# One block, two reserved tiles of expert 0, and the low parts of expert 0's first matrices computed ahead of the step plan

## What is computed

```python
def hier_moe(x, w_router_group, w_router_expert, moe_w1, moe_w3, moe_w2):
...
    p_grp = jax.nn.softmax((xt @ w_router_group).astype(jnp.float32), axis=-1)
    g_idx = jnp.argmax(p_grp, axis=-1)
...
    top_v, top_i = lax.top_k(e_logits, TOP_K_INNER)
    top_w = jax.nn.softmax(top_v, axis=-1) * g_gate
    expert_id = g_idx[:, None] * EXPERTS_PER_GROUP + top_i
...
    h = jax.nn.silu(jnp.einsum('nd,edf->nef', xt, moe_w1)) * jnp.einsum('nd,edf->nef', xt, moe_w3)
    h = h * gates.astype(h.dtype)[..., None]
    y = jnp.einsum('nef,efd->nd', h, moe_w2)
    return y.reshape(shp)
...
    x = layer_norm(ALPHA * x + m, ln1_g, ln1_b)
    x = layer_norm(ALPHA * x + hier_moe(x, w_router_group, w_router_expert, moe_w1, moe_w3, moe_w2),
                   ln2_g, ln2_b)
```

## Time and profile before

| what | us |
|---|---|
| median of three runs | 1213.25 (1211.74 to 1216.63) |
| profiled execution, first to last instruction | 1221.8 |
| end of the first block (PE L801, DVE goes on) | 750.3 |
| plan copied | 764.3 |
| output product of step 1 begins | 794.6 |
| PE busy | 1127.9 (92%) |
| DVE busy | 808.8 (66%) |
| ACT busy | 538.7 (44%) |

### The profile page before, as it was taken

The page is one execution under the profiler, slowest core; times in us unless marked ns, Lnnn a source line. Parts: engine busy times, 40 slices in busy tenths (PEclk is TensorE's granted clock), DMA queues, the critical chain, the costliest instruction groups (busy, mean ns, idle before and its releaser), DMA issues. The chain is left out here.

```text
span 1221.8 us, 20871 instructions
## 1 busy us (share of the span) xinstructions
PE 1127.9 (92%) x5734; PEld 998.6 (82%) x5735; DVE 808.8 (66%) x1530; ACT 538.7 (44%) x703; POOL 188.0 (15%) x189
## 2 busy tenths in 40 slices
PE   6999999999999999999999985899998999999970
PEld 6999999999999999788888864677887887777750
DVE  5666455464346556667777766866755798888884
ACT  4465344443344444323222224444544676656530
POOL 1000000000001001002223313315001033221322
PEclk9999999999999999999999997899998999999995
DMA  5331597768776444524444228676766789788563
GB/s 184 124 105 57 134 138 131 76 155 98 92 83 217 189 159 152 197 69 139 149 161 172 105 63 273 234 267 208 265 230 245 271 309 356 292 294 294 192 223 137
DMA packets 86989, 221.08 MB, mean 181 GB/s; under 512 B 18992, under 2 KB 45648, under 8 KB 80656
## 3 DMA queue, kind: packets, MB, share of 16 engines
q1 hardware_dynamic: 57824, 129.90, 32.3%
q0 software_dynamic: 18160, 59.53, 14.6%
q10 hardware_dynamic: 10944, 30.95, 13.5%
HBM read 133.75 MB, written 86.58 MB: 180 GB/s over the span
## 5 line engine op out<-in xcount | busy, mean ns | idle before, releaser
L1462 PE MATMUL ps_h<-x_hi,xt_hi 128*128 x320 | 128.6, 402 | 2.7 <-issue 1.8
L1462 PE MATMUL ps_h<-x_hi,xt_lo 128*128 x320 | 125.0, 391 | 0.0
L1462 PE MATMUL ps_h<-w_lo,xt_hi 128*128 x320 | 124.9, 390 | 0.0
L287 PE MATMUL ps_vb_c<-x_hi,w_hi 128*128 (+1 forms) x320 | 114.6, 358 | 10.6 <-DVE x_lo L461 10.6
L287 PE MATMUL ps_vb_c<-x_hi,w_lo 128*128 (+1 forms) x320 | 113.9, 356 | 0.0
L287 PE MATMUL ps_vb_c<-x_lo,w_hi 128*128 (+1 forms) x320 | 113.2, 354 | 0.0
L287 PE MATMUL ps_va_b<-x_hi,w_lo 128*128 (+1 forms) x320 | 112.7, 352 | 0.0
L287 PE MATMUL ps_va_b<-x_hi,w_hi 128*128 (+1 forms) x320 | 112.6, 352 | 0.0
L287 PE MATMUL ps_va_b<-x_lo,w_hi 128*128 (+1 forms) x320 | 111.8, 349 | 0.0
L1119 DVE TENSOR_TENSOR w_lo<-x_hi_p,x_hi 128x2048 f32 (+1 forms) x32 | 73.1, 2286 | 7.3 <-ACT x_hi L1114 5.6
L476 DVE SCALAR_TENSOR_TENSOR xc<-vb,par,xc 128x416 f32<-128x416 f32 (+1 forms) x60 | 39.1, 652 | 56.1 <-ACT xc L348 52.3
(11 more groups left out here) (356 smaller groups left out, 2656.1 us busy)
## 6 DMA issues: line engine op xcount, KB each, us to landing
x_hi_p<-in_w SPq DMA_DIRECT2D x48, 1024.0 KB, 5.1
o_scr<-x_raw ACTq DMA_DIRECT2D x42, 512.0 KB
w_lo_p<-xs_scr SPq DMA_DIRECT2D x41, 512.0 KB
o_scr<-w_lo_p SPq DMA_DIRECT2D x41, 512.0 KB
w_raw<-in_w_in POOLq DMA_DIRECT2D x19, 512.0 KB, 3.7
xs_scr<-x_raw ACTq DMA_DIRECT2D x17, 512.0 KB
x_raw<-in_x_t SPq DMA_DIRECT2D x20, 416.0 KB, 3.4
x_hi_p<-y_scr SPq DMA_DIRECT2D x16, 512.0 KB, 4.1
```

The source lines that it names most:

```text
L287: mm = pe.matmul(ps[i][:, 0:CHUNK], w[:, i, k], x[:, k, bass.ds(c * CHUNK, CHUNK)], start=(k == 0 and n == 0), stop=(k == KT - 1 and n == 2))
L1462: mm = pe.matmul(ps_h[par][:], x[:, par, k], w[:, bass.ds(at, 1), k].rearrange("p o n -> p (o n)"), start=(k == 0 and n == 0), stop=(k == ...
```

## The change

The two blocks become one: the engines' functions of the first phase (`project_*`) are called at the head of those of the second, with three hooks (`ahead`, `between`) through which work of the experts stands inside the first phase. Two tiles of expert 0 are reserved in place of one (FROZEN = 2), and both hidden products are computed with `first_part` ahead of the plan, the low parts of the matrix among them. SP loads both tiles' rows ahead of expert 0's matrices; the gates of the last two groups have a semaphore of their own (`s_gl`). On DVE `lo13` and the second `x_lo` stand ahead of `plan_steps`, `lo2` ahead of the copy of the plan. `later_experts` goes to step 1 and takes a scan and a subtraction over from `ranks`, which goes to step 2; `slots` goes to step 3, `records` and `needed` to step 4. Line numbers move by some ten lines.

```diff
+FROZEN = 2
...
-        dve.memset(self.start[:, 0:1], float(P))
-        self.then(dve, dve.tensor_scalar(self.run[:, 0:1], self.run[:, 0:1], float(P), None, ALU.max))
+        dve.memset(self.start[:, 0:1], float(FROZEN * P))
+        self.then(dve, dve.tensor_scalar(self.run[:, 0:1], self.run[:, 0:1], float(FROZEN * P), None, ALU.max))
...
-                                    self.wts[0:rows, t, c:c + 1], None).then_inc(self.s_gs, 16)
+                                    self.wts[0:rows, t, c:c + 1], None).then_inc(self.s_gs if n < len(GROUPED) - 2 else self.s_gl, 16)
...
-            sp.wait_ge(s_m, NT)
-            for half in (0, 1):
-                sp.dma_start(ew.raw_half(half), w13[0][:, half * (KT // 2):(half + 1) * (KT // 2)]).then_inc(ew.s_r13[half], 16)
-            sp.dma_start(ew.w2_raw[:], w2[0]).then_inc(ew.s_r2, 16)
-            sp.dma_start(ew.ln2[:], ln[:, 2:4]).then_inc(ew.s_ln2, 16)
-            sp.wait_ge(mx.s_st_out, 16)
-            for n in range(LAST - 5, LAST - 1):
-                sp.wait_ge(rt.s_sc[n % 4], rt.landed(n))
-            sp.wait_ge(rt.s_gs, 16 * TOPK * GROUPED[LAST - 1][0])
-
-        @block.tensor
-        def _(pe):
+        def project_tensor(pe, ahead):
...
+            ahead()
...
             scores(NT - 1)
...
+                if t == NT - 1:
+                    ahead()
                 act.wait_ge(s_tr, t + 1)
...
+            between()
             both_parts(NT - 1)
...
+            between()
             logits_out(NT - 1)
...
+            project_sync(sp)
+            for n in range(LAST - 5, LAST - 1):
+                sp.wait_ge(rt.s_sc[n % 4], rt.landed(n))
+            for par in range(FROZEN):
+                sp.dma_start(xg[:, par], xs_scr[par * P:(par + 1) * P, :]).then_inc(s_xg[par], 16)
+            sp.wait_ge(handover.s_m, NT)
+            for half in (0, 1):
+                load_weights(sp, 0, half)
+            load_weights(sp, 0)
+            sp.dma_start(ln2, ln[:, 2:4]).then_inc(ew.s_ln2, 16)
+            sp.wait_ge(rt.s_gs, 16 * TOPK * GROUPED[LAST - 1][0])
+            sp.wait_ge(handover.s_rt, NT)
             sp.dma_start(consts[:, 0:NCONST], consts_in).then_inc(s_con, 16)
-            sp.dma_start(gate[:, slot(0, 0)], g_scr[0:P, :]).then_inc(s_g[0], 16)
+            for par in range(FROZEN):
+                sp.dma_start(gate[:, slot(par, 0)], g_scr[par * P:(par + 1) * P, :]).then_inc(s_g[par], 16)
+            sp.wait_ge(handover.s_st_out, 16)
             sp.wait_ge(s_plan, 1)
             for n in (LAST - 1, LAST):
                 sp.wait_ge(rt.s_sc[n % 4], rt.landed(n))
-            ahead = [load(1, 1), load(2, 0)]
+            ahead = load(2, 0)
             next_weights(sp, 1)
-            sp.wait_ge(rt.s_gs, 16 * TOPK * NT)
-            load_gate(1, 1, 0, ahead[0])
-            load_gate(2, 0, 1, ahead[1])
+            sp.wait_ge(rt.s_gl, 16 * TOPK * (NT - GROUPED[LAST - 1][0]))
+            load_gate(2, 0, 1, ahead)
...
+            project_gpsimd(pool)
             for n in (LAST - 1, LAST):
                 rt.scatter(pool, n)
...
             def count_later():
 
                 pe.wait_ge(s_later, 1)
-                of = later.rearrange("p t e -> p (t e)")
-                pe.matmul(ps_o[1][:, 0:NT * NE], consts[:, C_TRI:C_TRI + P], of, start=True, stop=True)
-                pe.matmul(ps_o[0][:, 0:NT * NE], consts[:, C_ONE:C_ONE + P], of, start=True, stop=True).then_inc(s_cnt2, 1)
+                pe.wait_ge(s_plan, 1)
+                line, ones = (lambda t: t.rearrange("p e t -> p (e t)")), consts[:, C_ONE:C_ONE + P]
+                pe.matmul(line(below), consts[:, C_TRI:C_TRI + P], line(later), start=True, stop=False)
+                pe.matmul(line(below), ones, line(tot2), start=False, stop=True)
+                pe.matmul(total, ones, inc2[:, :, NT - 1], start=True, stop=True).then_inc(s_cnt2, 1)
...
-                if early(s, 1):
-                    count_later()
-                else:
+                if not early(s, 1):
...
-                if left:
+                if left and not early(s, 1):
                     hidden(s + 1, 1 - par, pe.value_load(plan[0:1, 0, bass.ds(s + 1, 1)], min_val=0, max_val=NE - 1))
-
-
-            rt.counts(pe, LAST, ps_c, squares[:, 1], squares[:, 2])
-            turn(0, 0, 0, squares[:, 0])
-
-            def first_part(x, w, there, count):
+                if isinstance(s, int) and s == 1:
+                    count_later()
...
+            def first_part(s, x, w, there, count):
 
                 pe.wait_ge(there, count)
                 for k in range(KT):
-                    mm = pe.matmul(ps_h[0][:], x[:, 0, k], w[:, first, k].rearrange("p o n -> p (o n)"),
+                    mm = pe.matmul(ps_h[s][:], x[:, s, k], w[:, first, k].rearrange("p o n -> p (o n)"),
                                    start=(there is s_xhi and k == 0), stop=(there is s_13lo and k == KT - 1))
                 return mm
 
+            def ahead():
+                pe.wait_ge(handover.s_s, NT)
+                turn(0, 0, 0, squares[:, 0])
+
+            project_tensor(pe, ahead)
+            turn(1, 1, 0, squares[:, 0])
             pe.wait_ge(ew.s_13hi, 2)
-            first_part(xt_hi, w13_hi, s_xhi, 1)
-
+            first_part(0, xt_hi, w13_hi, s_xhi, 1)
+            rt.counts(pe, LAST, ps_c, squares[:, 1], squares[:, 2])
+            first_part(0, xt_lo, w13_hi, s_xlo, 1)
+            first_part(1, xt_hi, w13_hi, s_xhi, 2)
+            first_part(1, xt_lo, w13_hi, s_xlo, 2)
+            for s in range(FROZEN):
+                first_part(s, xt_hi, w13_lo, s_13lo, 2).then_inc(s_h, 1)
             pe.wait_ge(s_con, 16)
             pe.wait_ge(s_vals, 1)
...
-            first_part(xt_lo, w13_hi, s_xlo, 1)
-            first_part(xt_hi, w13_lo, s_13lo, 2).then_inc(s_h, 1)
-            turn(1, 1, 0)
             pe.wait_ge(s_plan, 1)
             last, _ = steps(pe, step)
...
-                    x_hi(1, 1)
-                    residual(1, 1, 0)
...
+            project_scalar(act, lambda: x_hi(0, 0), lambda: ew.hi13(act, 0, first, (0,)))
+            ew.hi13(act, 0, first, (1,))
+            x_hi(1, 1)
             rt.gate_exp(act, LAST)
-
             act.wait_ge(rt.s_exp, LAST + 1)
             act.activation(idle[:], rt.gex[:, 0, 0:1], ACT.Silu)
-            x_hi(0, 0)
             ew.hi2(act, 0, first)
-            residual(0, 0, 0)
+            for s in range(FROZEN):
+                residual(s, s, 0)
...
+                if isinstance(s, int) and s == 1:
+                    later_experts()
                 if isinstance(s, int) and s == 2:
+                    ranks()
+                if isinstance(s, int) and s == 3:
                     slots()
-                if isinstance(s, int) and s == 3:
+                if isinstance(s, int) and s == 4:
                     records()
-                if isinstance(s, int) and s == 4:
                     needed()
...
-                then(dve.tensor_tensor(later, big, over, ALU.mult))
-                then(dve.tensor_reduce(last_e[:], later, AX.X, ALU.max))
+                then(dve.tensor_tensor(big, big, over, ALU.mult))
+                then(dve.tensor_reduce(last_e[:], big, AX.X, ALU.max))
                 then(dve.tensor_tensor(last_e[:], last_e[:], rt.small[:, C_INV - C_DEC:C_INV - C_DEC + NT], ALU.add))
-                dve.tensor_tensor(later, later, last_e[:].unsqueeze(2).broadcast_to((P, NT, NE)), ALU.is_equal).then_inc(s_later, 1)
+                then(dve.tensor_tensor(later.rearrange("p e t -> p t e"), big,
+                                       last_e[:].unsqueeze(2).broadcast_to((P, NT, NE)), ALU.is_equal))
+                line = lambda t: t.rearrange("p a b -> p (a b)")
+                then(dve.tensor_tensor_scan(line(inc2), consts[:, C_SEG:C_SEG + NT * NE], line(later), 0.0, ALU.mult, ALU.add))
+                dve.tensor_tensor(tot2, inc2, later, ALU.subtract).then_inc(s_later, 1)
...
+            project_vector(dve, lambda: x_lo(0, 0))
+            dve.wait_ge(handover.s_lo, NT + 1)
             rt.assign(dve, LAST)
             rt.places(dve, LAST, ps_c)
+            ew.lo13(dve, 0, first)
+            x_lo(1, 1)
             dve.wait_ge(s_con, 16)
             plan_steps()
-            x_lo(0, 0)
-            ew.lo13(dve, 0, first)
             ew.lo2(dve, 0, first)
-            later_experts()
+            copy_plan()```

In the order of the program this shows at three places. The first is PE's list from the last tile's scores (L946 before, L937 after) to the step plan's matmuls (L1505, L1520) and step 0; `ps_cnt` is the bank of the counts, `ps_x` that of a transposed tile, `ps_h` the hidden product. Before:

```order
L946 MATMUL ps_l<-stack,parts 128x20
L801 UNCONDITIONAL_BRANCH
L1423 UNCONDITIONAL_BRANCH
L746 MATMUL ps_cnt<-r_both,x_lo_p 128x32
L747 MATMUL ps_cnt<-r_both,x_lo_p 128x32
L1429 MATMUL ps_x<-x_lo_p,w_lo_p 128x128 x8
L1494 MATMUL ps_h<-x_hi,xt_hi 128x512 x8
L1505 MATMUL ps_cnt<-consts_sb,vals 1x59 x4
```

136 lines of the change are left out of this document (72 added, 64 removed).

## The result

| kernel | median, us | ratio to before, 95% interval |
|---|---|---|
| before | 1214.28 (4 runs, 1211.74 to 1216.63) | |
| changed | 1225.35 (4 runs, 1223.02 to 1225.99) | 1.0093 [1.0074, 1.0112] |

The changed kernel is 11.1 us slower. 1218.6 was forecast, with 1210 to 1225 as the range: the sign came out, the size is twice the forecast, and the time lies 0.35 us outside the range. The profiled execution of the changed kernel took 1223.02 us, its span is 1221.3. (A run takes 1.7 us more than its span in every kernel here. The profile of before, with a span of 1221.8, was then a long execution, some 9 us over the median; its stretch that the change touches was less than 0.4 us longer than the mean of five.)

A forecast was written before the change was run, and what follows sets the result against it. PE (92% busy) was taken to bound the kernel, the seam being its largest gap. 4.1 us up to step 1's output plus 1.2 in later steps, 5.3 on the 1213.25 median, gave 1218.6 us, range 1210 to 1225.

The forecast's parts named there:

- term 6: Steps after step 1: +1.2 us, from `slots` replacing `records` in step 3 (+1.0) and 0.2 in step 4.
- the edits that were counted at nothing: Zero fill of one more tile in the mixer, the gates' own semaphore, 41 steps as before: 0 us.
- Start of the assignment: At the seam: barrier gone, but half 0 of `hi13` stands ahead of `parts` on ACT; -0.1 us, bounds -3.2 to +1.7.
- Counts: Counts read at the seam, behind eight hi·hi matmuls that need both matrix halves: +2.2 us, to 758.3.
- Plan: Plan copied at 774.6 instead of 764.3, +10.3 us, behind `lo13`, `x_lo` and 24 matmuls; bounds 772.9 and 778.1.
- Plan to hidden values: From plan to step 1's hidden values 13.2 us instead of 23.0, work now being ahead; net +0.5 us, at 787.8.
- Step 1: `later_experts` on a full DVE, then `count_later` ahead of PE's output: output at 798.7, +4.1 us in all.
- Rival B: Slower than the sum: gates' scatters delay half 1 to 754, half clock through all 24 matmuls; 1225 us, chance 0.17.
- Rival A: Matrices come early, halves by 743.5 and 749.5, clock up: hidden values 7.0 us early; 1211 us, chance 0.14.
- C: Seam neutral, step 1 not lengthened because `later_experts` fits while PE is in its hidden product; 1215 us, chance 0.19.

The follow-up runs named there:

- The experiment with the counts first: Changed kernel with plan, `later_experts` and `slots` early; also `parts` ahead of half 0 of `hi13` on ACT, counts ahead of PE's first hidden product: ratio 1.0050 to before.
- The two edits of step 3 above: Changed kernel with `later_experts` and `slots` early in step 1: 1.0052; kernel before with `records` moved from step 3 to step 4: 0.9988.
- the experiment in which step 1 goes first: Changed kernel with `later_experts` and `slots` early, plus step 1's silu, hidden values and output ahead of splitting expert 1's matrices: ratio 1.0032 to before.

## Why the prediction was wrong

The direction and the route to step 1 were right. Two steps of the sum failed: term 6, which priced the longer wait in step 3 and not the clock behind it, and the edits that were counted at nothing, where the end of the program grew by 1.9 us. Term by term:

1. **Start of the assignment** (-0.1 forecast, 1.2 in the mean, within the bounds of -3.2 to 1.7). As put: the barrier's wait was exchanged for one on the matrix. The experiment with the counts first shows the price of the order on ACT, 3.9 us; it bought nothing there, because the plan then waited for the constants.
2. **Counts** (2.2, 2.9). As put: behind half 1 of the matrix and eight matmuls at half clock (3.62 us; 3.60 was taken).
3. **Plan** (10.3, 12.0; in the profile of after 9.8). As put, in the bounds of 8.6 to 13.8. PE waits 4.38 us for `x_lo`, and the matmuls behind it run at both clocks. The other executions are 1.8 to 3.4 us later than the first.
4. **Plan to hidden values** (13.2 us, measured 13.2 in after and in the mean). The sum came out in part by luck, since two parts are off and cancel: rows were there after 3.8 us, not 4.5, and the transposes took 1.97, not 1.03. The 0.5 became 2.2 because the plan was late by more.
5. **Step 1** (3.6 more, 4.3 in the mean). The size nearly held, the mechanism only in part. `later_experts` took 3.5 us and ended at 792.56 as one of two nearly equal paths; the other, which ended last (793.53), was PE itself, at the lower clock at first. The forecast had left PE out of this sum: it had 5.6 us for a hidden product from the earlier trace rows, at the full clock, where this one took 7.3. As the sign it had named an idle PE of 3 to 5 us; there is none. Only in one of the four executions did PE wait, 0.59 and 0.35 us.
6. **Later steps** (1.2, measured 2.7). This term failed. A longer wait in step 3 was right (3.85 for 2.60, 1.25 us; the output product of step 3 is 1.3 us later in the mean), but it was priced as a wait. Its second price is the clock: the whole output product runs at 1.05 us per pair, where in before only half of it did, and step 4's output is later by another 1.0. The two edits of step 3 above confirm it: with `slots` or `records` taken out of that step the wait and the lower clock are both gone. The remaining 0.4 us is in step 2, where the exchange of `ranks` for `slots` was counted at nothing.
7. **"The other edits at nothing"**: 1.9 us at the end of the program, the second term that failed. 1.0 of it is POOL's drain, 7.58 us for 6.60, in every kernel of one block; what sets its length stays open. The other 0.9 is as large as executions differ there.

Terms 1 to 4 account for 1.7 us of the miss, term 5 for 0.7, term 6 for 1.5, the end for 1.9. Another 1.0 us between 1218.6 and 1225.35 is the base: the median of before rose from 1213.25 to 1214.28 with a fourth run.

Rival B gave the measured time, 1225, and is nevertheless refuted by the rows: it decided from 753 for half 1, which came at 751.0, and its plan at 780.1 came at 774.1. Rival A needed half 1 at 749.5. C is refuted by `count_later` ahead of the output and by 11.36 us from hidden values to output (783.06 to 794.42) where before had 7.27 (787.37 to 794.64). Its picture of DVE is what the rows show all the same: in after, `later_experts` (789.05 to 792.56) fits into PE's hidden product (786.25 to 793.53), because that product ran at the lower clock.

The Trainium skill's rule that was weighed ("TensorE: Matmul & The Clock Gate", section "HAM oscillation — how this bites in real kernels": matmuls between waits start at the low clock) agrees with the rows of step 1 and step 3, behind waits of 2.85 and 3.85 us. It does not hold behind every wait of this case: in the experiment in which step 1 goes first, the transposes behind a wait of 3.00 us for a DMA took 1.09 us, the full clock. The forecast applied the rule to the plan's matmuls alone, where both clocks were seen, and not to the two steps in which the change made a wait longer; there the rows show some 2 us and 1 us of it.

## What to carry to other kernels

Work put into a step can have two prices: the wait that it makes for the next engine, and the clock at which that engine then works; read the durations behind each wait, not only the wait. And moving work into an empty stretch gains nothing while the stretch behind it waits for something else: before a plan or a matrix is moved, ask which of the two releases the next step, and test that by moving it alone.

## What was not expected of the hardware

- Waits of PE of two to four microseconds were mostly followed by the lower clock. Behind 1.67 us in step 1 the transposes took 1.09 us, behind 2.85 they took 1.97, with the hidden product's first matmuls at 0.63 instead of 0.39. In step 3, behind 2.72 us, three of six pairs went at 1.05; behind 3.85 all six. But behind the 3.00 us of the kernel with step 1 first the clock did not fall, so that the length of one wait does not tell it alone. Two microseconds of vector work moved out of that step removed wait and half clock together.
- The end of the program took 1.0 us longer after POOL's last scatter in every kernel of one block: POOL's drain at the block's end, 7.58 us for 6.60. Why it is longer was not tested.
- Executions of one kernel differ by several microseconds in an unchanged part (group 6's first scatter at 723.7 to 736.9 us in five profiles of before); the ratios of alternating runs are certain to 0.2 to 0.5% all the same.
